# Part of the prompt's indexer sum moved to the matmul engine by diagonal weights

## What is computed

```python
dots = jnp.einsum('bthd,bsd->bths', qi, ki_all) * (D_IDX ** -0.5)      # 8 heads of 64
score = jnp.einsum('bth,bths->bts', wi, jax.nn.relu(dots))             # wi: a weight per query and head
causal = jnp.arange(L)[None, :] <= q_pos[:, None]
score = jnp.where(causal[None], score, -jnp.inf)
vals, sel = lax.top_k(score, topk)                                     # 256 keys a query
```

## Time and profile before

| what | value |
|---|---|
| median of 3 runs | 4034.18 us (4029.04 to 4034.57) |
| the profiled execution | 4031.83 us, its span 4030.0 us |
| PE busy over the span | 3565.0 us, 88% |
| DVE, ACT, POOL busy | 2783.3, 2215.7, 1055.3 us |
| mean granted TensorE clock | 0.937 of 2.4 GHz |
| stage of the change | 1037.4 to 1328.6 us, 291.2 us |

### The profile page before, as it was taken

How to read it: one execution, slowest core, us unless ns; L and a number is a source line. 1 busy time by engine, 2 the same in 40 slices (tenths; PEclk the granted TensorE clock), 3 DMA queues, 4 the chain that set the end, 5 groups by cost and what they waited for, 6 DMA issues and landing times. The chain is left out here.

```text
span 4030.0 us, 53421 instructions
## 1 busy us (share of the span) xinstructions
PE 3565.0 (88%) x18411; PEld 2848.2 (71%) x18411; DVE 2783.3 (69%) x4729; ACT 2215.7 (55%) x3701; POOL 1055.3 (26%) x1135
## 2 busy tenths in 40 slices
PE   8999998779777488874599998979999999999998
PEld 7778787767655245443488886868888887888886
DVE  6675756767888789888678885665566554555565
ACT  3343424666678589887577674345455444443232
POOL 0000001755211011100256730215556551000011
PEclk9999999999878699996799999989999999999999
DMA  6555454535200244423456633667667656554464
GB/s 167 179 149 163 141 161 127 155 113 161 60 21 21 73 157 168 161 102 113 128 191 223 223 124 132 201 222 219 188 226 231 196 185 194 183 183 147 139 215 139
DMA packets 394574, 633.11 MB, mean 157 GB/s; under 512 B 98072, under 2 KB 220792, under 8 KB 386008
## 3 DMA queue, kind: packets, MB, share of 16 engines
q1 hardware_dynamic: 315368, 316.50, 26.2%
q0 software_dynamic: 78544, 313.43, 23.3%
q10 hardware_dynamic: 416, 0.02, 0.0%
HBM read 448.87 MB, written 180.96 MB: 156 GB/s over the span
## 5 line engine op out<-in xcount | busy, mean ns | idle before, releaser
L3832 PE MATMUL up_acc<-x_parts_first,w_up_parts 128*128 128x512 f32 x1536 | 359.2, 393 | 15.3 <-DVE w_up_parts L3582 15.3
L775 PE MATMUL accumulated<-hT,w_in_parts 128*128 128x512 f32 x1536 | 361.4, 395 | 3.2 <-DVE w_in_parts L509 3.2
L3832 PEld LDWEIGHTS up_acc<-x_parts_first,w_up_parts 128*128 128x128 f32 x1536 | 291.8, 190 | 77.3 <-DVE w_up_parts L3582 16.2
L775 PEld LDWEIGHTS accumulated<-hT,w_in_parts 128*128 128x128 f32 x1536 | 290.6, 190 | 66.4 <-DVE w_in_parts L509 4.9
L2818 DVE TENSOR_SCALAR_CACHE_REDUCE junk_dve<-score,candidate 128x2048 bf16<-128x2048 f32 (+6 forms) x224 | 328.5, 1505 | 9.2 <-DVE candidate L2804 8.7
L3923 PE MATMUL down_acc<-w_down_parts_even,hidden_parts 128*128 128x512 f32 x1344 | 315.7, 393 | 12.5 <-DVE hidden_parts L3618 10.2
L3923 PE MATMUL down_acc<-w_down_parts_odd,hidden_parts 128*128 128x512 f32 x1344 | 312.7, 390 | 0.0
L3923 PEld LDWEIGHTS down_acc<-w_down_parts_even,hidden_parts 128*128 128x128 f32 x1344 | 254.1, 190 | 66.9 <-issue 14.0
L2741 ACT ACTIVATE junk_act<-score,candidate 128x1920 bf16<-128x1920 f32 (+6 forms) x224 | 286.5, 1295 | 20.9 <-DVEq L2805 17.0
L3923 PEld LDWEIGHTS down_acc<-w_down_parts_odd,hidden_parts 128*128 128x128 f32 x1344 | 251.9, 188 | 53.2 <-issue 1.0
L3384 ACT ACTIVATE hidden_parts<-hidden_raw 128x1024 fp32r<-128x1024 f32 x112 | 118.6, 1059 | 310.6 <-PE down_acc L3923 289.3
(11 more groups left out here) (550 smaller groups left out, 8661.6 us busy)
## 6 DMA issues: line engine op xcount, KB each, us to landing
hidden_raw<-scratch_hs POOLq DMA_DIRECT2D x112, 512.0 KB, 4.6
w_in_raw<-in_w_in SPq DMA_DIRECT2D x80, 512.0 KB, 4.1
up_raw<-scratch_ws SPq DMA_DIRECT2D x128, 256.0 KB, 2.9
scratch_hs<-hidden_even POOLq DMA_DIRECT2D x112, 256.0 KB, 4.9
scratch_hs<-hidden_odd POOLq DMA_DIRECT2D x112, 256.0 KB, 5.0
up_raw<-in_w_up SPq DMA_DIRECT2D x96, 256.0 KB, 5.7
weight_sums<-in_w_down POOLq DMA_DIRECT2D x16, 1024.0 KB, 5.3
scratch_wt<-weight_sums POOLq DMA_DIRECT2D x16, 1024.0 KB, 6.0
```

The source lines that it names most:

```text
L775: mm = pe.matmul(z, w2[:, g % 2, b, k2 * ST + n * P:k2 * ST + (n + 1) * P], h[:, a, k, :], start=(first and j == 0), stop=(last and j == 2))
L3832: mm = pe.matmul(up_bank(n), wp[:, n % SLOTS, b, q * P:(q + 1) * P], X(i)[:, a, q, :], start=(q == 0 and (a, b) == (0, 0)), stop=(q == QUA ...
```

## The change

The weighted sum of heads 0 to 2 over the first 512 columns of each chunk is formed on PE. For each tile and each of these heads POOL multiplies the identity by the column of 128 weights (`spread_weights`, a matrix with the weights on its diagonal), and PE multiplies it with the rectified dots in `R`, adding the three heads up in one PSUM bank `first_heads` (`add_on_pe`, plain fp32; the matmul for unit u-2 follows the dots of unit u). DVE then does for heads 0 to 2 only the columns past 512, or nothing but a semaphore increment where the chunk is no wider; head 3 takes its near half from `first_heads` and its far half from the score; heads 4 to 7 are as before. `RB` goes from 3 to 4, and a buffer of `R` is free only when the matmul has read it too. The bank for `first_heads` is that of the bias: the eight turned biases now go to the upper bank of the dots' buffers during narrow chunks (heads 0, 2, 4 of the rest chunks of tiles 8 to 11), and PE waits before a later wide unit until DVE has copied them. SP loads the identity first.

```diff
+    ON_PE = 3
-        RB, DB = 3, 3
+        RB, DB = 4, 3
+        LAG = 2
...
-        pc, bt = ps("folded_counts", [P, ST])[:, 0:1], ps("bias_turned", [P, ST])[:, 0:SKEW]
+        pc, part = ps("folded_counts", [P, ST])[:, 0:1], ps("first_heads", [P, ST])
+        ident, spread = sb("identI", [P, P]), sb("wi_spread", [P, 2, ON_PE, P])
+        id_in, spread_rdy, part_done = sem("i_ident"), sem("i_spread"), sem("i_part")
...
-        head_at = {24 + 14 * h: h for h in range(HEADS)}
+        narrow = [u for u, (i, c, w, h) in enumerate(UNITS) if w <= ST and i >= 8 and h in (0, 2, 4)]
+        head_at = {u: h for h, u in enumerate(narrow[:HEADS])}
+
+        def bt(h):
+            return dots[:, narrow[h] % DB, ST:ST + SKEW]
...
+        def on_pe(upto):
+            return sum(1 for i, c, w, h in UNITS[:max(upto, 0)] if h < ON_PE)
...
+                sp.dma_start(ident[:, :], io["ident"]).then_inc(id_in, 16)
...
+                def spread_weights(n):
+                    if n >= 2:
+                        pool.wait_ge(q_lo, n - 1)
+                        pool.wait_ge(part_done, on_pe(tile_end[n - 2]))
+                    for h in range(ON_PE):
+                        pool.tensor_scalar(spread[:, n % 2, h, :], ident[:, :], wi[:, SEARCHED[n], h:h + 1], None, ALU.mult).then_inc(spread_rdy, 1)
+
+                pool.wait_ge(id_in, 16)
+                spread_weights(0)
+                spread_weights(1)
                 for n in range(2, NSRCH):
...
+                    spread_weights(n)
...
+                def add_on_pe(u):
+                    i, c0, wide, h = UNITS[u]
+                    if h >= ON_PE:
+                        return
+                    n, w = SEARCHED.index(i), min(ST, wide)
+                    pe.wait_ge(relu_done, u + 1)
+                    if h == 0:
+                        pe.wait_ge(spread_rdy, ON_PE * (n + 1))
+                        if u:
+                            pe.wait_ge(acc_done, u - IH + ON_PE + 1)
+                    pe.matmul(part[:, 0:w], spread[:, n % 2, h, :], R[:, u % RB, 0:w], start=(h == 0), stop=(h == ON_PE - 1)).then_inc(part_done, 1)
...
                     if u >= DB:
                         pe.wait_ge(relu_done, u - DB + 1)
+                    turned = sum(1 for v in head_at if v < u)
+                    if wide > ST and turned:
+                        pe.wait_ge(bt_rdy, turned)
...
                     mm.then_inc(dots_done, 1)
+                    if u >= LAG:
+                        add_on_pe(u - LAG)
                     if u in head_at:
                         pe.wait_ge(b_wide, 2)
-                        pe.wait_ge(bt_rdy, head_at[u])
-                        pe.matmul(bt, rbw[:, head_at[u], :], boh[:, :], start=True, stop=True).then_inc(bt_ps, 1)
+                        pe.wait_ge(bt_rdy, sum(1 for v in head_at if v <= u - 2 * DB))
+                        pe.matmul(bt(head_at[u]), rbw[:, head_at[u], :], boh[:, :], start=True, stop=True).then_inc(bt_ps, 1)
...
                     if u >= RB:
                         act.wait_ge(acc_done, u - RB + 1)
+                        act.wait_ge(part_done, on_pe(u - RB + 1))
...
+                    near, far = slice(0, min(ST, wide)), slice(ST, wide)
+                    w = wi[:, i, h:h + 1]
                     dve.wait_ge(relu_done, u + 1)
-                    if h == 0:
-                        dve.tensor_scalar(s, r, wi[:, i, h:h + 1], None, ALU.mult).then_inc(acc_done, 1)
+                    dve.wait_ge(acc_done, u)
+                    if h < ON_PE and wide <= ST:
+                        dve.sem_inc(acc_done, 1)
+                    elif h == 0:
+                        dve.tensor_scalar(s[:, far], r[:, far], w, None, ALU.mult).then_inc(acc_done, 1)
+                    elif h < ON_PE:
+                        dve.scalar_tensor_tensor(s[:, far], r[:, far], w, s[:, far], ALU.mult, ALU.add).then_inc(acc_done, 1)
+                    elif h == ON_PE:
+                        dve.wait_ge(part_done, on_pe(u))
+                        adds = [dve.scalar_tensor_tensor(s[:, near], r[:, near], w, part[:, near], ALU.mult, ALU.add)]
+                        if wide > ST:
+                            adds.append(dve.scalar_tensor_tensor(s[:, far], r[:, far], w, s[:, far], ALU.mult, ALU.add))
+                        adds[-1].then_inc(acc_done, 1)
                     else:
-                        dve.wait_ge(acc_done, u)
-                        dve.scalar_tensor_tensor(s, r, wi[:, i, h:h + 1], s, ALU.mult, ALU.add).then_inc(acc_done, 1)
+                        dve.scalar_tensor_tensor(s, r, w, s, ALU.mult, ALU.add).then_inc(acc_done, 1)
```

2 lines of the change are left out of this document (1 added, 1 removed).

## The result

The changed kernel takes **4047.74 us** (median of 7 runs, 4043.62 to 4058.71 without one disturbed run) where the kernel before takes 4032.36 (7 runs): a ratio of 1.0038, 95% interval 1.0028 to 1.0048, about 15 us slower. 4027 was forecast, 7 us faster: the direction was wrong. The time lies inside the range of 4008 to 4050 only because that range takes in rival (b) with its 4048, which described another mechanism, as the experiments show. The profiled execution has a span of 4045.6 us (before 4030.0).

A forecast was written before the change was run, and what follows sets the result against it. DVE was taken to bound the stage that scores the prompt's keys. Terms of -28 (DVE's work), +9 (search loop), +4 (POOL) and +8 (clock) gave -7 us, 4027 from the median; range 4008 to 4050.

The forecast's parts named there:

- rival (b): Key-scoring stage: PE at 1.2 GHz becomes the bound; at 8 cold rounds +14 us, 4048; chance 0.23.
- part 5: Moved bias turns and buffers: PE's wait for copies 0 to 3 us, taken as 0; fourth buffer 0 to 5.
- part 1: DVE in the scoring stage: multiplies and adds of heads 0 to 3 that go, minus 28 us (23 to 31).
- Part 2: PE in the scoring stage: 66 plain fp32 matmuls, 53 us at 2.4 GHz, 104 at 1.2; hidden at 2.4 only.
- Part 3: Search loop through ACT's count, PE's fold and DVE's update: wins in eleven of 32 rounds, plus 9 us (0 to 15).
- part 6: PE's clock in the scoring stage: fewer falls, each costing more; plus 8 us (0 to 35).
- Rival (c): Scoring stage: the loop through count, PE and fold sets the pace, DVE's gain becomes waits; +3 us, 4037; chance 0.17.
- Part 4: POOL's 42 weight multiplies can hold up DVE adds, plus 4 us (0 to 14); SP's identity DMA charged nothing.

The follow-up runs named there:

- e5: e1 with the diagonal matmul in one-pass fp32r instead of plain fp32; 4023.79 us, ratio 0.9969 to the kernel before.
- e1: The changed kernel with two bias turns instead of three in each narrow chunk of tiles 8 to 11; 4034.54 us, ratio 0.9999 to the kernel before.
- e15: e1 with five heads instead of three on the diagonal, still four-pass matmuls; ratio 1.0008 to the kernel before.
- e12: e5 with five heads instead of three on the diagonal; median 4017.88 us, ratio 0.9955 to the kernel before.
- e6: e1 with POOL's weight multiplies left out for all but the first two tiles (wrong weights later); ratio 0.9999 to the kernel before.
- e13: The changed kernel, packed bias included, with only the diagonal matmul in one-pass fp32r; ratio 0.9992 to the kernel before.
- e10: The changed kernel without the eight bias matmuls, DVE copying other data, all waits kept; ratio 1.0025 to the kernel before.
- e14: e10 also without PE's wait for DVE's copies ahead of wide chunks; ratio 1.0000 to the kernel before.
- e7: The kernel before with four relu buffers (`RB` = 4) and nothing else; ratio 0.9988 to the kernel before.
- e2: The kernel before with only the bias turns moved as in the change, three buffers, all heads on DVE; ratio 1.0004 to the kernel before.

## Why the prediction was wrong

The step that failed is part 5: the packed bias and the wait for its copies were put at nothing, and they cost 12 us. Without them the gain of part 1 is lost to waits as well, a little more than parts 3, 4 and 6 allowed. The prediction's sum for the stage was -28 + 9 + 4 + 8 = -7; the profile shows +11.8. (Its reading of the page was loose too: the digits of PE fall to 4 and not only to 7 in the first half. Nothing hangs on that.) By its parts:

**Part 1, DVE's work (right).** -28 forecast with bounds of 23 and 31; busy time went from 259.4 to 234.1, -25.3. The 1024-wide adds are 40, as said. The near add with a PSUM operand takes 747 ns, as long as the SBUF one (751): the 0.72 taken for its step was too low.

**Part 2, PE's new work (right).** 0.87 us at 2.4 GHz was taken for 512 columns. In the timeline a diagonal matmul starts at 1312.38 and the fold behind it at 1313.24, 0.86. In e5 it is 0.24 (1280.11 to 1280.35). The Trainium skill's page "FP8 and Floating Point Precision", section "TensorE Precision Notes", has true FP32 as four passes through the array; the steps in these traces are in a ratio of 3.6, near to it.

**Part 3, the loop through count, PE and fold, and part 6, the clock (undersized).** Together with part 4 they were put at 21 us. Measured without the bias' wait, DVE's waits grew by 26 (e1: 36.9 against 10.6). The prediction looked at the loop of the search alone, round by round, and let it win in eleven rounds. It left out that head 3's near add waits for the same queue: 13.8 us in e1, more than the fold's growth of 9.1. Rival (c), "DVE's gain turns into waits", comes nearest, but it too names only the fold and the rectified units. Its test, waits for the fold and for ACT under 25 us, failed in the changed kernel (36.5); in e1, without the packed bias, they are 23.1 and would have passed. Only with the wait for PE's sum (50.7 and 36.9) is the loss of the gain seen.

**The clock (right sign, wrong role).** Its mean rose from 0.77 to 0.88 as hoped. That the time is rival (b)'s 4048 is a coincidence. Its sign, a clock of 0.85 or less, isn't there, and e1 has nearly the same clock (0.90) and none of the loss. Nor does the mean clock order the kernels: e15 has the highest (0.94) and a long stage, and e5 and e12 have a lower one than e1 (0.79 and 0.86) and are the fast ones. Single stretches at the lower clock do cost, as rival (b) says: at 1219.84 a diagonal matmul takes 1.91 (a granted clock of 0.53 from 1215 to 1222) and DVE waits 5.65, and the bias matmuls above take 1.64. What such stretches cost in sum was not measured by itself.

**Part 4, POOL and SP (price wrong, effect too small to tell).** A multiply was put at 0.15 to 0.33 us, as an eighth of wider instructions; it takes 0.87 on average and 0.59 in the first round (3.53 for six at 1039.40). Eight of them take 4.7 to 7 us, where the cast of 1024 columns that they were divided from takes 1.2, so dividing by the width was no price for them. "Each can hold up a DVE add" is the other way round in the traces, and e6 finds no cost that can be told from nothing, or from the 4 us forecast. "Nothing is charged" for the late first weights was wrong in one place: PE waits 1.60 for them at 1041.33, and round 0 is 2.3 us longer (part 3 had charged 4 to it for another reason).

**Part 5, the bias (the step that failed).** "0 to 3 us, taken as 0." The packed bias costs 12.0 us of the stage and 16 timed (the change against e1), 9 timed with the short diagonal matmul (e13 against e5), and it alone turns no change into a loss. That the wait by itself can cost this much is shown by e10 against e14 (10 us timed), which have no bias matmuls; how the change's own 12 us are split between the wait and the matmuls ahead of fold and dots stays open. The argument was that the narrow units take 0.4 us each and ACT may lead by one more buffer. Three things were wrong in it. The wait was priced by the units that lie between, and not by when DVE would reach its copy; DVE's queue ahead of the copy holds two adds that last 3.3 us beside POOL's query conversion, which stood in the earlier trace rows, was counted in the sum of before, and was not carried over to this wait. While PE waits it forms nothing, so ACT and then DVE run dry as well; without the wait both work through the hold-up, as e14's timeline shows. And "same instructions" left out that three bias matmuls of 1.64 us now stand within one narrow chunk, ahead of a fold and of dots that DVE soon runs out of. What part 5 says of the fourth buffer, 0 to 5 us, agrees with e7 (about 5).

With the measured terms: e1 has -25 of DVE's work, +26 of waits (PE's queue, stretches at the lower clock, the first round and POOL together) and 1 less in short gaps, which is 0 (its stage is 0.2 us under that of before); the packed bias adds 12. Of the 19 us between forecast and profile 12 are thus part 5, 4 are parts 3, 4 and 6 and 3 are part 1. The 3.8 us outside the stage exceed the 1 us that the prediction allowed, but, as shown at the start, so does the spread of these executions.

**Still open.** How the 12 us of the packed bias are split between its matmuls and the wait; how much of the 26 us in e1 is PE at the lower clock; why rounds 17 and 20 swing between profiles; and whether fold first helps in the one-pass version.

## What to carry to other kernels

Price a new wait by what stands on the awaited engine's queue ahead of the instruction that it waits for, with every known hold-up of those, and by who runs dry behind the waiting engine; a guard that is free at most places can cost 10 us at the two where the pipeline's lead is spent. Work taken from the busiest engine comes back as time only if the engine that takes it over stays short in its queue: with five heads moved, a matmul of 0.24 us left the kernel 18 us faster (about 5 of them the fourth buffer's, by e7) and one of 0.86 not faster at all. And when a change brings several things along (a buffer, a moved table), run each alone, but also take each out of the finished change. Alone the buffer showed its 5 us, while the moved table showed next to nothing (e2); only taking it out of the change (e1) showed that it cost 12 to 16 us there.

## What the runs showed of the hardware

In the changed kernel a GpSimd multiply of 128x128 by a per-partition scalar takes 0.59 us in the first six and up to 1.51 later, when it begins beside one of VectorE's adds of two SBUF operands (42 of them, mean 0.87), where the 128x1024 cast mostly takes 1.04. A VectorE add with one operand in PSUM is no faster or slower than one from SBUF (747 and 751 ns at 512 columns), but copying 384 columns out of PSUM takes 0.55 us and out of SBUF 0.35 (in e14). A 512-column matmul of plain fp32 steps 0.86 us and one of fp32r 0.24, both at the higher clock. The granted clock fell when PE had less to do (0.90 in e1, 0.79 in e5) and the kernel was faster all the same, so the clock alone says nothing of a change's worth.
